# Latent attention's projections: third latent chunk in banks 6 and 7, sums inside chunks, rotary query parts first

## The reference

```python
def mla_shared_kv(h, kv_in_g, w_dkv, kv_norm_g, w_kr, w_uk, w_uv, cos, sin):
    hn = rms_norm(h, kv_in_g)
    c_kv = rms_norm(hn @ w_dkv, kv_norm_g)               # 256 latents
    k_rope = apply_rope(hn @ w_kr, cos, sin)             # 64
    k_nope = (c_kv @ w_uk).reshape(b, s, 8, 128)
    v = (c_kv @ w_uv).reshape(b, s, 8, 128)

def mla_attention(hn, w_dq, q_norm_g, w_uq, ...):
    q = (rms_norm(hn @ w_dq, q_norm_g) @ w_uq).reshape(b, s, 8, 192)   # 384 latents
    q_nope, q_rope = q[..., :128], apply_rope(q[..., 128:], cos, sin)
    ... scores, softmax, values by blocks of 128 queries
```

## Time and profile before

| | |
|---|---|
| median of 3 runs | 2027.05 us (2026.63 to 2028.33) |
| the profiled execution | 2025.48 us, its span 2023.7 us |
| mean granted clock of TensorE | 0.993 |
| TensorE busy | 1944.8 us (96%) |
| VectorE, ScalarE, GpSimd busy | 830.7, 765.4, 676.2 us |
| DMA | 169.41 MB, mean 84 GB/s |

### The profile page before, as it was taken

How to read it: one execution, slowest core, us unless ns; L and a number is a source line. 1 busy time by engine, 2 the same in 40 slices (tenths; PEclk the granted TensorE clock), 3 DMA queues, 4 the chain that set the end, 5 groups by cost and what they waited for, 6 DMA issues and landing times.

```text
span 2023.7 us, 25099 instructions
## 1 busy us (share of the span) xinstructions
PE 1944.8 (96%) x9954; PEld 1610.3 (80%) x9954; DVE 830.7 (41%) x1369; ACT 765.4 (38%) x1127; POOL 676.2 (33%) x205
## 2 busy tenths in 40 slices
PE   5998999999997899999999999999999999999999
PEld 4665978888896768988888897778888798888887
DVE  5897721111275264611121376756553242212122
ACT  5564432222344352522231356763344333212121
POOL 2783044434402310143444303222121403443442
PEclk9999999999999999999999999999999999999999
DMA  4211242222211211222222312111112222222222
GB/s 164 84 42 64 78 120 84 104 97 97 97 68 37 89 42 43 84 104 90 101 101 87 117 59 84 63 47 58 43 53 104 94 104 84 104 84 104 104 78 89
DMA packets 30247, 169.41 MB, mean 84 GB/s; under 512 B 3619, under 2 KB 5956, under 8 KB 13252
## 3 DMA queue, kind: packets, MB, share of 16 engines
q1 hardware_dynamic: 30148, 168.00, 23.5%
HBM read 162.22 MB, written 5.77 MB: 83 GB/s over the span
## 4 chain that ended last, share of the span: by engine, by line
PE 85%; DVE 7%; ACT 3%; POOL 2%; DMA 2%; issue 1%; SPq 0%; POOLq 0%; DVEq 0%; ACTq 0%
PE ps L1974 58%; PE ps L1995 8%; PE ps L2322 4%; PE ps L2388 3%; POOL wlo L491 2%; PE ps L2085 1%; DMA wraw<-stream 1%; PE ps L2479 1%; ACT whi L559 1%; PE ps L2491 1%; PE ps L2228 1%; PE ps L2229 1%; PE ps L2489 1%; PE ps L2056 1%; DVE ps L1332 1%
## 5 line engine op out<-in xcount | busy, mean ns | idle before, releaser
L491 POOL TENSOR_TENSOR wlo<-wraw,whi 128x2048 fp32r<-128x2048 f32 (+4 forms) x146 | 604.9, 4144 | 1288.1 <-ACT whi L559 1288.1
L559 ACT ACTIVATE whi<-wraw 128x2048 fp32r<-128x2048 f32 (+4 forms) x161 | 281.5, 1748 | 394.4 <-PE ps L1974 360.7
L1974 PE MATMUL ps<-xh,whi 128*128 128x512 f32 x1044 | 414.2, 397 | 16.7 <-POOL wlo L491 10.4
L1974 PE MATMUL ps<-xh,wlo 128*128 128x512 f32 x1044 | 408.3, 391 | 0.0
L1974 PE MATMUL ps<-xl,whi 128*128 128x512 f32 x1044 | 408.0, 391 | 0.0
L1974 PE MATMUL ps<-hh,whi 128*128 128x512 f32 x752 | 295.3, 393 | 7.1 <-DVE hl L1418 6.6
L1974 PE MATMUL ps<-hh,wlo 128*128 128x512 f32 x752 | 293.3, 390 | 0.0
L1974 PE MATMUL ps<-hl,whi 128*128 128x512 f32 x752 | 293.3, 390 | 0.0
L1974 PEld LDWEIGHTS ps<-xh,whi 128*128 128x128 f32 x1044 | 197.2, 189 | 64.7 <-POOL wlo L491 13.5
L1974 PEld LDWEIGHTS ps<-xl,whi 128*128 128x128 f32 x1044 | 197.2, 189 | 42.7 <-issue 2.4
L1974 PEld LDWEIGHTS ps<-xh,wlo 128*128 128x128 f32 x1044 | 196.9, 189 | 41.7
(11 more groups left out here) (325 smaller groups left out, 2865.0 us busy)
## 6 DMA issues: line engine op xcount, KB each, us to landing
wraw<-stream SPq DMA_DIRECT2D x132, 1024.0 KB, 4.8
wraw<-stream SPq DMA_DIRECT2D x12, 768.0 KB, 4.1
wraw<-stream SPq DMA_DIRECT2D x6, 384.0 KB, 3.2
resid<-x SPq DMA_DIRECT2D x4, 512.0 KB, 7.2
wraw<-stream SPq DMA_DIRECT2D x8, 256.0 KB, 2.9
branch_scratch<-RS SPq DMA_DIRECT2D x8, 256.0 KB, 2.1
wraw<-stream SPq DMA_DIRECT2D x4, 512.0 KB, 3.5
out<-resid SPq DMA_DIRECT2D x4, 512.0 KB, 2.6
```

The lines of the kernel that those rows point to most:

```text
L491: pool.tensor_tensor(wlo[:, p, 0:w], wraw[:, p, 0:w], whi[:, p, 0:w], ALU.subtract).then_inc(lo_ready, 1)
L559: act.activation(whi[:, p, 0:w], wraw[:, p, 0:w], ACT.Copy).then_inc(hi_ready, 1)
L1974: ins = pe.matmul(ps[:, 2 * p + n, :], wt[:, p, w], xt[:, k0 + k, :], start=k == 0 and q == 0, stop=k == k_tiles - 1 and q == 2)
```

## The change

What it does, edit by edit:

- Latent chunk 2 (46) is written to banks 6 and 7 (`LATENT_BANK`), so it needn't wait for a pair. The sum of squares of the inputs goes to bank 4 in this boundary (`PRE_SUMS` by boundary). Its matmul is taken out of latent chunk 1 and hooked into chunk 2, ahead of place (0, 4); the kv sums are hooked ahead of place (1, 2).
- The `wlo` of chunk 46 and of chunk 51 (the first of uq) are made by VectorE: the first inside the adding tree after its first add, the second in the q norm ahead of the third tile's product. `weights_low` itself moves outward unchanged. ScalarE rounds chunk 46 ahead of the last four squares.
- uq's chunks are put in another order: the two rotary chunks first, then the four others (the stream's order, and the copies' destinations, follow). The four rotations are hooked into uq chunks 2, 3 and 4. The key's rotation moves from before uk to after the q sums.
- ScalarE's order is rewritten: the q squares one at a time between copies, the rounding of chunk 51 inside the q splits, both copies of uk 2 and 3 behind them; the roundings of the first two wo chunks behind all V copies.

```diff
-BY_DVE = {c + i for c in LAST for i in range(3)}
+BY_DVE = {c + i for c in LAST for i in range(3)} | {START["latent"] + 2, START["uq"]}
...
-        presum, PRE_SUMS = NT[:, 0, :], 6
+        presum, PRE_SUMS = NT[:, 0, :], (6, 4, 6, 6, 6)
+        LATENT_BANK = 6
...
                 if i == FFN0:
                     for j in range(DT):
                         high(1, j, 1)
+                    head(last + 3)
                 pre_squares(1)
...
-            head(START["latent"] + 2)
             pre_root_of(FFN0)
...
             root("kv", KV_LORA, eps_rms)
             split_heads("kv", lambda j: xh[:, j, :], 2)
+            emptied(act, c0 + 1)
+            square("q", E[:, 3, :], 0)
             head(c0 + 4)
             emptied(act, c0 + 2)
-            for m in range(4):
-                if m == 0:
-                    square("q", E[:, 3, :], 0)
-                    square("q", E[:, 4, :], 1)
-                if m == 2:
-                    square("q", E[:, 5, :], 2)
-                    root("q", Q_LORA, eps_rms)
-                    split_heads("q", lambda j: xh[:, 2 + j, :], 3)
-                copy_pair(START["uk"] + m, Z[:, 2 * m:2 * m + 2, :])
-                head(START["uk"] + m + 2)
+            square("q", E[:, 4, :], 1)
+            c = START["uk"]
+            copy_pair(c, Z[:, 0:2, :])
+            head(c + 2)
+            square("q", E[:, 5, :], 2)
+            copy_pair(c + 1, Z[:, 2:4, :])
+            head(c + 3)
+            root("q", Q_LORA, eps_rms)
+            split_heads("q", lambda j: xh[:, 2 + j, :], 1)
+            head(c + 4)
+            split_heads("q", lambda j: xh[:, 2 + j, :], 2, 1)
+            copy_pair(c + 2, Z[:, 4:6, :])
+            copy_pair(c + 3, Z[:, 6:8, :])
+            head(c + 5)
             for m in range(6):
-                copy_pair(START["uq"] + m, Y[:, 2 * m:2 * m + 2, :] if m < 4 else
-                          (SQ[:, :, :] if m == 4 else rope_raw))
+                copy_pair(START["uq"] + m, (SQ[:, :, :], rope_raw)[m] if m < 2 else Y[:, 2 * m - 4:2 * m - 2, :])
                 head(START["uq"] + m + 2)
...
-                head(c + 2)
+                if m < 2:
+                    head(c + 2)
+            head(START["wo"])
+            head(START["wo"] + 1)
...
+                        if (n, half, i) == (4, 0, FFN0):
+                            weights_low(last + 3)
...
-            normed_pair(START["latent"] + 2, E[:, 4:6, :])
+            normed_pair(START["latent"] + 2, E[:, 4:6, :], LATENT_BANK)
             norm_split("q", lambda j: E[:, 3 + j, :], lambda j: vec("q_norm", j), lambda j: xh[:, 2 + j, :],
-                       lambda j: xl[:, 2 + j, :], 3)
+                       lambda j: xl[:, 2 + j, :], 3,
+                       between=lambda j: weights_low(START["uq"]) if j == 2 else None)
...
-                                 midway=((1, 4 if two else 0), pre_sums) if half else None)
+                                 midway=((1, 0), pre_sums) if half and not two else None)
+                return pre_sums
...
-            ffn(0)
+            latent_sums = ffn(0)
...
             c = START["latent"]
-            stats("kv")
-            project(c + 2, hh, hl)
-            emptied(pe, c + 1)
-            pe.wait_ge(tables_loaded, 16)
-            pe.matmul(ps[:, 6, :], rotate, E[:, 2, :], start=True, stop=True).then_inc(rotated, 1)
+
+            pe.wait_ge(lo_ready, c + 3)
+            project(c + 2, hh, hl, hooks={(0, 4): latent_sums, (1, 2): lambda: stats("kv")}, start=False,
+                    bank=LATENT_BANK)
...
             for m in range(4):
                 project(START["uk"] + m, xh, xl, k_tiles=2, need=operand("kv") if m == 0 else None)
                 if m == 1:
                     stats("q")
+                    emptied(pe, c + 2)
+                    pe.wait_ge(tables_loaded, 16)
+                    pe.matmul(ps[:, 6, :], rotate, E[:, 2, :], start=True, stop=True).then_inc(rotated, 1)
+            turns = {2: {(0, 1): lambda: turn_rope(0), (1, 1): lambda: turn_rope(1)},
+                     3: {(1, 0): lambda: turn_rope(2)}, 4: {(0, 2): lambda: turn_rope(3)}}
             for m in range(6):
-                project(START["uq"] + m, xh, xl, k_tiles=3, k0=2, need=operand("q") if m == 0 else None)
-            for r in range(4):
...
+                project(START["uq"] + m, xh, xl, k_tiles=3, k0=2, need=operand("q") if m == 0 else None,
+                        hooks=turns.get(m, {}))
```

More of the change, by code:

```diff
@@ L524, in _ @@
             rest(DT + 1)
-            for c, n in runs(DT + 2, N_CHUNK, [c + i for c in LAST for i in (0, 3)]):
+            for c, n in runs(DT + 2, N_CHUNK, [c + i for c in LAST for i in (0, 3)] + [START["uq"] + 1]):
                 if c in BY_DVE:
@@ L657, in pre_root_of @@
                 act.wait_ge(pre_summed, i + 1)
-                sums = ps[:, PRE_SUMS, :]
+                sums = ps[:, PRE_SUMS[i], :]
                 step(act.activation(sums, sums, ACT.Ln, scale=1.0 / D, bias=eps_rms))
@@ L1952, in project @@
             def project(c, hi, lo, h=0, k_tiles=DT, k0=0, need=None, second=None, second_need=None,
-                        paired=True, midway=None, hooks={}, start=True):
+                        paired=True, midway=None, hooks={}, start=True, bank=None):
                 if start:
@@ L2030, in pre_sums @@
                     pe.wait_ge(pre_added, 2 * i + 2)
-                    pe.matmul(ps[:, PRE_SUMS, :], ones, Z[:, 0, :], start=True, stop=True).then_inc(pre_summed, 1)
+                    pe.matmul(ps[:, PRE_SUMS[i], :], ones, Z[:, 0, :], start=True, stop=True).then_inc(pre_summed, 1)
                 for half in range(2):
@@ L2529, in pre_sums @@
                 pe.wait_ge(pre_added, 2 * OUT + 2)
-                pe.matmul(ps[:, PRE_SUMS, :], ones, Z[:, 0, :], start=True, stop=True).then_inc(pre_summed, 1)
+                pe.matmul(ps[:, PRE_SUMS[OUT], :], ones, Z[:, 0, :], start=True, stop=True).then_inc(pre_summed, 1)
             _, _, lo_sem, base = pre_norms(OUT)[0]
@@ L2577, in pack @@
     c, w = START["uq"], a["mla_w_uq"][0].reshape(Q_LORA, NH, QKD)
+    for m in range(2):
+        put(c + m, w[:, 4 * m:4 * m + 4, NOPE:QKD].reshape(Q_LORA, 256))
     for m in range(4):
[L2579 to L2581 removed]
+        put(c + 2 + m, w[:, 2 * m:2 * m + 2, 0:NOPE].reshape(Q_LORA, 256))
     w = a["w_in_2"][0]
```

50 lines of the change are left out of this document (21 added, 29 removed).

## The result

The changed kernel takes 2009.75 us in the median of 10 runs (2004.22 to 2017.13), the one before 2026.77 (10 runs, 2024.06 to 2034.34). The ratio is 0.9918, 95% interval 0.9904 to 0.9933: 17 us, 0.8% faster. The forecast was 2007.5, in 2004.5 to 2011.5.

A forecast was written before the change was run, and what follows sets the result against it. TensorE, busy 96% of the span, was taken as the bound. Of 24.2 us lost in the stretch 4.6 stay: gain 19.6, from 2025.5 to 2005.9, plus 1.6 to the median, 2007.5 us; range 2004.5 to 2011.5.

The forecast's parts named there:

- The budget: Boundary's end to first attention score: 93.1 us, of which 68.9 is TensorE work and 24.2 lost; 4.6 would stay.
- Step 1: Sum of squares and latent chunk 2: the tree's 5.9 us stand, 1.8 of clock and 1.4 kv stand go.
- The charge of 0.2 us for thin margins: Around latent chunk 2 and the kv sums: 0.2 us charged because three places have only 0.1 to 0.4 us to spare.
- Step 2: uk and the q norm: a 1.9 us stand before uq stays, for 3.3 before, waiting for uk 2's copy.
- The clock term: Behind the remaining stand before uq: no clock loss taken, 0 us, with 2.0 as the other end.
- Step 3: Rotations inside uq: their stands go, 0.1 us charged for the lock (other end 3.5); uv starts 0.8 us late.
- Step 4: Before attention: pause 1.3 us instead of 2.1; wo roundings ahead of the first exponential charged 0.2 (ends 0 and 1.9).
- The first: Clock falls after the 1.9 us stand before uq: + 2.0, 2009.5 us, up to 2011; chance 0.22.
- The second: Locked port holds GpSimd's query subtractions or thin margins break: 3 to 6 us stay, 2010.5 to 2013.5; chance 0.13.
- The third: Better than forecast: stand before uq shorter, starting costs hidden, 2003 to 2005.5 us; chance 0.08.
- The fourth: Chunk 2 still stands for the sum by 5.8 us, VectorE's subtraction queuing ahead of the adds: 2015; chance 0.03.
- The fifth: Slower than before: lower clock somewhere in the 1318 us after the first score, 40 us gives 2047; chance 0.02.

The follow-up runs named there:

- pool_46: The changed kernel with the subtraction for latent chunk 2 on GpSimd again instead of VectorE; median 2010.27 us of 4 runs, stretch 2.1 us more.
- copy_first: The changed kernel with uk 2's copy moved ahead of the last two q splits on ScalarE; median 2007.17 us of 8 runs, stretch 1.4 us less.
- wo_early: The changed kernel with the first two wo chunks' roundings back between the V copies; median 2013.75 us of 6 runs, stretch 0.2 us more.
- the longer stand: The changed kernel with uk 2's copy behind uk 3's copy and uq 1's rounding; median 2014.64 us of 10 runs, stretch 3.3 us more.

## Why the prediction came out as it did

**The budget** came out as the sum said: first score at 685.71, forecast "near 686"; gain in the stretch 19.9 us, forecast 19.8 before the charge in attention. Part of that is luck. Left over in the stretch are idle times of 1.55 us before uq, 0.2 and 0.15 at uv, and 1.1 before attention. The forecast counts a stand from where the next matmul would have issued, 0.16 us before the last record ends. Counted so, they are 1.7 (forecast 1.9), 0.4 and 0.3 (0.8 together) and 1.3 (1.3), in all 3.7, where the forecast had 4.4 with its small charges. The 68.9 us of work in turn took 0.6 us more: uq with its four rotations ran from 643.73 to 672.18 without a stand, 28.45 us for the 27.9 of the sum. The two misses cancel.

**Step 1** was right in each of its times: tree done at 616.50 (forecast 616.9), sum at 616.88 (617.0), kv sums 621.87 (622.0), chunk 2 over at 627.6 (627.9). The charge of 0.2 us for thin margins wasn't needed. The runs with it undone give it 11.0 us of the stretch, more than half of the change: 6.7 of stands and the rest of clock. Its argument holds in part. The held add explains the tree's late end, but once the sum stands behind twelve matmuls of chunk 2 the tree is no longer waited for, with the lock or without it (`pool_46`); of what was undone alone, it is the place of the sum that brings the most, 5.6 us.

**Step 2.** The remaining stand was named with its releaser (uk 2's copy, shown by `copy_first`) and was 0.2 us too long in the sum, counted alike. The clock term was the right choice: the stand of 1.55 us was followed by no fall in any of the seven profiles that have it. But the argument was weaker than it read. The row at 1681.8, 2.63 us with the clock at 1.00 behind it, was one draw: the same stand was followed by a fall in 7 of 14 profiles. And the trace at hand had two more stands of this length, 2.50 us before 51.9 and 2.48 before 686.15, both with a fall behind them, which the argument left out.

What the step didn't see is that the moved subtraction of chunk 51 is itself a cost of 1.3 us. I had it in the chain, 1.0 us between uk 2's end and the copy, and didn't ask what the chain would be without it.

**Step 3.** No wait at the rotations; undoing them costs 4.3 us of stretch, of which 1.7 at most are clock. The lock showed where I had put it and was hidden, as said. VectorE's cosine product beside GpSimd's subtraction in the changed kernel:

```profile
654.62 1.95 DVE L1536 TENSOR_TENSOR NT<-SQ,Z 128x512 f32<-128x512 f32 x1
...
666.15 1.21 DVE L1536 TENSOR_TENSOR NT<-Z 128x512 f32<-128x512 f32 x1
```

GpSimd's subtractions at the same places:

```profile
645.43 2.35 POOL L492 TENSOR_TENSOR wlo<-wraw,whi 128x768 fp32r<-128x768 f32 x1 [7.88 <-ACT whi L560]
...
654.18 1.85 POOL L492 TENSOR_TENSOR wlo<-wraw,whi 128x768 fp32r<-128x768 f32 x1 [2.32 <-ACT whi L560]
```

The product takes 1.95 and 1.21 us for 0.69, and GpSimd's first uq subtraction, beside the key's turn, 2.35 for 1.85. The Trainium skill (SBUF — State Buffer, SBUF: two separate sides) says that whichever of the two starts first holds the pair for its whole instruction and the other is blocked. The rows agree: the product of 654.62 starts behind GpSimd's 654.18 and is held, and GpSimd's subtraction of 645.43 starts behind VectorE's product of 645.39 and is longer by 0.5 us. I had charged 0.1 us, with 3.5 as the other end; it was 0.

**Step 4.** The pause before attention went from 1.9 to 1.1 us, and attention's start has 1.14 us of stands for 1.08. With `wo_early` the two orders differ by 0.2 us. My charge of 0.2 was 0.1; right, and unimportant.

**The median** is where the forecast is 2.3 us off, inside its range. I set the sum against the profiled run (2005.9; it was 2005.5) and carried over the 1.6 us by which the profiled run of before lay under its median. For the changed kernel that distance is 4.3 us. The step that failed is this last one: the distance between one profiled run and the median isn't a constant of the setup. It is mostly clock lost elsewhere, and differs from run to run. That the profiled run itself came out at 2005.5 for 2005.9 is luck to that extent: the two profiled runs happened to lose the same outside the stretch, 6.1 and 6.3 us of clock, and the changed kernel's second profile, with the same stretch, is of a run of 2012.5. Over all runs with their clock listed (76 of the kernel before, 16 of the changed one) the mean span splits so:

| | time at full clock | lost to the lower clock | span |
|---|---|---|---|
| before | 2009.3 | 17.1 | 2026.4 |
| changed | 1998.3 | 10.7 | 2009.0 |
| gain | 10.9 | 6.4 | 17.4 |

This split gives the clock too much, for part of its lower level lies in the stands. So in the tree's stand of the kernel before, where TensorE is busy for 0.00 us:

```profile
615.60:618.60 3.00, 0.00 (x0) 0.00 (x0) 2.96 (x2) 0.00 (x0) 2.12 (x1) 0.50 0.00 0
```

Of the 8.5 us of clock lost in that stretch, TensorE was busy for 6.4. So of the 19.9 us gained there about 6.4 are clock and 13.5 are stands.

The runs spread by 12 us and more in both kernels. In the five profiles of runs that lie 2.5 us or more above their kernel's median, no clock is lost in the stretch and 11 to 21 us outside it, for 6.3 in the changed kernel's first profile.

The mean gain, 17.4 us, is below the 20.0 of the two profiles. Outside the stretch the kernel before lost about 8.6 us (17.1 less the 8.5 that its stretch lost in both profiles), the changed one 10.7; over the 50 runs of this and the other kernels whose profiled stretch lost none it is 11.0. The standard errors are 0.5 and 0.7. So it is likely, but not shown, that some 2 us of the gain are given back as clock in the rest of the program.

**Not undone.** Step 1 (11.0), the longer stand (3.3), the rotations (4.3) and the wo roundings (0.2) make 18.8 of the 19.9 us. No run gives chunk 2 its old banks alone, or uq its old order, so what these two edits bring by themselves isn't shown.

**The rivals.** The first, the clock after the 1.9 us stand, didn't come. The second, lock and margins, showed as records and cost nothing. The third, a stand before uq that is shorter than forecast, came by 0.2 us of stand, too little to count. The fourth: no wait at the sum. The fifth, slower by a clock that falls in the rest of the program: falls there are, up to 10 to 12 us near 1206 us, in 7 of 12 profiles of changed kernels. The two profiles of the kernel before show none at the same stage, near 1225, but it has runs up to 2041.7, and where these lose their time was not seen. So this rival is refuted as far as it said slower than before; that the change costs a little there stays open.

## What to carry over

Budget a stretch by its matmuls at full clock and ask what of the rest each edit removes; the starts that such a sum gives held to 0.5 us here, and the stand that stays can be named beforehand. Work on the bottleneck's pauses first where they are long, for they often carry a second price in clock; and when a weight or operand subtraction is moved to VectorE to escape the lock, look at what queues behind it there. Two misses that cancel look like a sum that is right: compare it term by term, each counted the same way. Compare kernels that differ by a few microseconds by span times granted clock, since the time of one run, or of one profile, can lie 12 us off for reasons elsewhere.

## What the runs showed of the hardware

**The price of a stand is partly a draw, and its length alone doesn't tell the odds.** TensorE's stands of over 1.4 us, and one shorter, with the profiles in which the clock fell around them, of all that have them:

| stand | place | a fall |
|---|---|---|
| 1.26 us | near 755 or 773 | 2 of 14 |
| 1.5 us | near 267, 842 and 1357 | 0 of 14 at each |
| 1.55 us | before uq | 0 of 7 |
| 1.4 to 1.9 us | before chunk 2 (`pool_46`), before attention, near 280 | 0 of 6 |
| 1.93 to 2.25 us | near 51 | 0 of 5 |
| 2.45 to 2.50 us | near 51 | 8 of 9 |
| 2.47 us | near 279 (`copy_first`) | 1 of 1 |
| 2.48 us | at the rotations, 672 or 686 | 3 of 3 |
| 2.5 to 2.6 us | near 145 | 2 of 14 |
| 2.63 us | near 1662 or 1682 | 7 of 14 |
| 3.1 to 3.2 us | before uq | 2 of 3 |
| 3.66 us | near 21 | 0 of 14 |
| 3.87 and 5.8 us | the tree | 4 of 4 |
| 6.6 us | near 177 | 14 of 14 |

The short one of 1.26 us, before 753.92 in `copy_first`:

```profile
753.60:757.00 3.40, 3.08 (x15) 3.08 (x16) 0.26 (x1) 0.60 (x1) 0.00 (x0) 0.50 0.00 0
```

Stands of about 2.5 us fared quite differently by place. A fall cost 1.7 us at the least, 3.4 to 5.1 around the longest. The Trainium skill (TensorE: Matmul & The Clock Gate, What's actually happening) says that the gate's looks aren't tied to the kernel's start, and that the same kernel therefore fares differently from run to run; the stands with both outcomes agree. What sets the odds of a place stays open.

**The clock can stay low under full work.** In `copy_first` it fell near 1207 us, behind a stage of 136-column matmuls whose longest stand is 0.6 us, and then:

```profile
1208.00:1228.00 20.00, 20.00 (x69) 16.17 (x69) 6.38 (x12) 8.17 (x11) 4.53 (x1) 0.50 0.15 52
```

Seven of the 12 profiles of changed kernels lost 3.4 to 11.9 us there, the others nothing. What decides it stays open: no run changed that stage.

**The lock lengthens the GpSimd side too.** GpSimd's subtraction of 2048 columns took 5.03 us beside the tree in `pool_46`, where the median of its kind is 4.60 (and 4.49 in the earlier trace rows, where it held the add and wasn't held itself); that of 768 took 2.35 us beside VectorE's key turn and 1.83 to 1.85 elsewhere.
